# Expert layer in units of 32 rows on four column quarters of TensorE, where it was 64 rows on two column halves

## The reference, cut to what matters

```python
def moe_ffn(h, router_w, router_b, w_gate_up, b_gate_up, w_down, b_down):
    logits = (xt @ router_w + router_b)              # xt: 512 tokens x 1024
    top_v, top_i = lax.top_k(logits, TOP_K)          # 4 of 32 experts each
    gates = jax.nn.softmax(top_v, axis=-1)
...
    def expert_block(args):                          # for the rows of one expert
        gu = xb @ w_gate_up[e] + b_gate_up[e]        # 1024 -> 2048
        x_glu = jnp.minimum(gu[:, ::2], SWIGLU_LIMIT)
        x_lin = jnp.clip(gu[:, 1::2], -SWIGLU_LIMIT, SWIGLU_LIMIT)
        act = x_glu * jax.nn.sigmoid(SWIGLU_ALPHA * x_glu) * (x_lin + 1.0)
        return act @ w_down[e] + b_down[e]           # 1024 -> 1024
```

## Time and profile before

| | us |
|---|---|
| median of 3 runs | 1922.38 (1922.17 to 1924.41) |
| span of the profiled execution (first to last instruction) | 1919.6 |
| expert stage, from SP's first transfer in it to the last matmul's end | 360.7 to 1521.35 |
| PE busy in the span | 1788.8 |
| DVE, ACT, POOL busy | 1025.5, 795.8, 236.5 |

### The profile page before, as it was taken

One profiled execution on the slowest core, in us unless ns is written; L12 is line 12 of the kernel. 1 busy time (PEld: TensorE's weight loads), 2 busy tenths in 40 slices (PEclk: granted clock), 3 DMA queues, 4 the chain that ended last, 5 costly groups with the idle time before them and its releaser, 6 DMA issues. The chain is left out here.

```text
span 1919.6 us, 41921 instructions
## 1 busy us (share of the span) xinstructions
PE 1788.8 (93%) x14459; PEld 1106.8 (58%) x14459; DVE 1025.5 (53%) x1632; ACT 795.8 (41%) x1163; POOL 236.5 (12%) x302
## 2 busy tenths in 40 slices
PE   6999888599999999999999899999999769998897
PEld 3999654455555555555554455555555336777763
DVE  5794435554554555544544345545454473874655
ACT  5335523244444444444443344444444433533411
POOL 0000000111111111111111011111111220350000
PEclk9999999699999999999999899999999879999999
DMA  8881771449878997997599998999999662221011
GB/s 328 271 263 45 197 236 43 180 158 406 356 284 318 423 379 284 363 427 324 206 406 427 426 427 338 421 427 372 405 427 426 260 211 68 77 77 46 21 40 44
DMA packets 129708, 520.06 MB, mean 271 GB/s; under 512 B 13618, under 2 KB 52291, under 8 KB 80355
## 3 DMA queue, kind: packets, MB, share of 16 engines
q1 hardware_dynamic: 116754, 483.41, 64.3%
q0 software_dynamic: 12736, 35.17, 4.9%
q10 hardware_dynamic: 146, 0.48, 0.1%
HBM read 494.10 MB, written 24.90 MB: 270 GB/s over the span
## 5 line engine op out<-in xcount | busy, mean ns | idle before, releaser
L1893 DVE COPY ring<-staging 128x2048 f32 (+1 forms) x385 | 475.2, 1234 | 506.8 <-PE banks L1754 307.8
L1754 PE MATMUL banks<-ring,rowsT 128*64 128x256 f32 x6144 | 700.9, 381 | 3.2 <-ACT rowsT L1843 3.2
L1754 PEld LDWEIGHTS banks<-ring,rowsT 128*64 128x64 f32 x6144 | 443.4, 138 | 310.5 <-issue 78.7
L1825 ACT ACTIVATE ring<-staging 128x2048 f32 (+1 forms) x193 | 369.0, 1912 | 338.6 <-PE banks L1754 274.7
L1780 PE MATMUL banks<-ring,hiddenT 128*64 128x512 f32 x1536 | 375.4, 610 | 0.5 <-PEq L1811 0.3
L1780 PEld LDWEIGHTS banks<-ring,hiddenT 128*64 128x64 f32 x1536 | 93.7, 137 | 137.3 <-issue 113.0
L1831 ACT ACTIVATE glu<-banks 128x128 f32<-128x128 f32 x192 | 53.2, 277 | 281.5 <-DVE lin L1899 281.5
L601 PE MATMUL banks<-w_in_hi,hT 128*128 128x256 f32 (+1 forms) x768 | 147.3, 291 | 1.6 <-issue 1.6
L2227 PE MATMUL banks<-h3T,w_in_hi 128*128 128x512 f32 x400 | 130.5, 408 | 1.4 <-DVE h3T L2403 1.4
L601 PEld LDWEIGHTS banks<-w_in_hi,hT 128*128 128x128 f32 x768 | 122.5, 194 | 3.6 <-issue 3.5
L1707 POOL DMA_DIRECT2D expert_rows<-y_rows x94 | 52.4, 558 | 532.5 <-ACT y_rows L1849 531.5
(11 more groups left out here) (413 smaller groups left out, 1796.6 us busy)
## 6 DMA issues: line engine op xcount, KB each, us to landing
staging<-in_w_gate_up SPq DMA_DIRECT2D x250, 1024.0 KB, 12.6
staging<-in_w_down SPq DMA_DIRECT2D x128, 1024.0 KB, 12.6
stage<-in_w_mod SPq DMA_DIRECT2D x21, 1024.0 KB, 6.1
stage<-in_w_in SPq DMA_DIRECT2D x25, 512.0 KB, 4.1
expert_rows<-y_rows POOLq DMA_DIRECT2D x94, 128.0 KB, 5.8
stage<-in_w_in SPq DMA_DIRECT2D x11, 1024.0 KB, 6.2
expert_rows<-catT SPq DMA_DIRECT2D x1, 7936.0 KB
early<-in_w_gate_up SPq DMA_DIRECT2D x6, 1024.0 KB, 11.2
```

Of the source, the lines that this page charges most:

```text
L1754: mm = pe.matmul(k.bank(j % 2)[c * SLOTS:(c + 1) * SLOTS, 0:UP], rowsT[:, kk, half, :], w[:, kk * WIDE + c * UP:kk * WIDE + (c + 1) * UP], ...
L1825: act.activation(ring[:, pos % RING, :], staged(e, c), ACT.Copy).then_inc(act_filled, 1)
L1893: dve.tensor_copy(ring[:, pos % RING, :], staged(e, c)).then_inc(dve_filled, 1)
```

## The change

SLOTS goes from 64 to 32, so the counts above give 80 units: 6 experts with one, 14 with two, 7 with three, 2 with four, 2 with five, and one with seven. A unit's 32 rows stand on four groups of 32 array columns (`QUARTERS`); each quarter has a quarter of the output features, and reads its own quarter (`PART` = 512 floats) of every chunk. The weights are laid out anew on the host so that a chunk of gate and up holds 128 input features for all outputs, and chunks come in the order 0 to 7 (up), 8 to 11 (down). The down part of unit i - 1 now stands behind the whole up part of unit i. The hidden rows of a unit are made in one go, and the column that picks the expert's bias comes from the router (`k.lane`) instead of a load for each unit. POOL fetches rows two units ahead and no longer loads `picked`; its store is one transfer instead of two. The first expert's early chunks are copied to the ring from where they were loaded. SP's loads are written out one by one, without a loop. The router's one-hot matrices have 512 columns. `gate2` goes through HBM to make room.

The core of the diff:

```diff
-SLOTS = 64
+SLOTS = 32
+QUARTERS = 4
...
-BY_DVE = (0, 2, 3, 5, 6, 8, 9, 11)
-BY_ACT = (1, 4, 7, 10)
+BY_DVE = (0, 1, 3, 4, 6, 8, 9, 11)
+BY_ACT = (2, 5, 7, 10)
...
 # SP
+                def free(c, last):
+                    filled(sp, last if c < KT else last + 1, c)
...
 # POOL
                 def store_rows(n):
                     pool.wait_ge(y_read, n)
-                    for part in range(2):
-                        pool.dma_start(rows_of(part, n * SLOTS - SLOTS), y[part * SLOTS:(part + 1) * SLOTS, :]
-                                       ).then_inc(y_out, 16)
-                    pool.wait_ge(y_out, 32 * n)
+                    pool.dma_start(store_of(n * SLOTS - SLOTS), y[:]).then_inc(y_out, 16)
+                    pool.wait_ge(y_out, 16 * n)
                     pool.sem_inc(y_free, 1)
-                gather(0)
-                load_picked(0)
-                load_picked(1)
+                gather(0, y, 1)
                 gather(1)
+                gather(2)
                 with pool.Fori(1, units) as i:
-                    load_picked(i + 1)
-                    gather(i + 1)
+                    gather(i + 2)
                     store_rows(i)
...
 # PE
+                def up(i, qs=range(KT)):
...
+                        for c in range(QUARTERS):
+                            w = ring[:, q % RING, c * PART:(c + 1) * PART]
+                            mm = pe.matmul(k.bank(0)[c * SLOTS:(c + 1) * SLOTS, :], rowsT[:, q % 2, row], w,
...
+                with pe.Fori(1, units) as i:
+                    up(i)
+                    down(i - 1, i)
+                    turn_hidden(i)
+                    turn_rows(i + 2)
+                    add_bias(i + 1)
...
 # ACT
+                with act.Fori(1, units) as i:
+                    e = expert_on(act, i)
+                    fill(i, e, 5)
+                    fill(i, e, 7)
+                    fill(i, expert_on(act, i - 1), 10)
+                    gate(i)
+                    rows_turned(i + 1, i * CHUNKS + KT)
+                    fill(i + 1, expert_on(act, i + 1), 2)
+                    read_y(i - 1, i * CHUNKS + CHUNKS)
+                    hidden_turned(i)
...
 # DVE
+                with dve.Fori(1, units) as i:
+                    e = expert_on(dve, i)
+                    fill(i, e, 3)
+                    fill(i, e, 4)
+                    pick_expert(i + 1)
+                    fill(i, e, 6)
...
+                    fill(i, e_before, 8)
+                    fill(i, e_before, 9)
+                    linear(i)
+                    fill(i, e_before, 11)
+                    finish_hidden(i)
```

More of the change, by code:

```diff
@@ L41 @@
 TABLE = ENDS + NE + LINE
-UP = 2 * P
-NM = 8
 CHUNK = 2048
@@ L1673, in _ @@
[L1673 to L1679 removed]
+                up = lambda e, q: d["w_gate_up"][(e * KT + q) * P:(e * KT + q + 1) * P, :]
+                down = lambda e, m: d["w_down"][(e * 4 + m) * P:(e * 4 + m + 1) * P, :]
@@ new lines, in _ @@
+                for m in range(EARLY - AHEAD):
+                    arrived(m)
+                for m in range(EARLY, NE * CHUNKS):
+                    e, c = m // CHUNKS, m % CHUNKS
+                    old = m - STAGED
+                    if old >= 0:
+                        if old % CHUNKS == 0 or old == 0:
+                            of = old // CHUNKS
+                            last = sp.value_load(k.table[0:1, ENDS + of:ENDS + of + 1], min_val=0, max_val=NBLK - 1)
+                        free(old % CHUNKS, last)
+                    sp.dma_start(staging[:, m % STAGED * CHUNK:(m % STAGED + 1) * CHUNK],
+                                 up(e, c) if c < KT else down(e, c - KT)).then_inc(raw_in[m % STAGED], 16)
+                    arrived(m - AHEAD)
@@ L1811, in _, with add_bias @@
-                pe.sem_inc(chunk_done, 2)
-                down(end + 3, units, 3)
+                def add_bias(i):
+                    pe.wait_ge(pick_ready, i + 1)
+                    first = not (isinstance(i, int) and i == 0)
+                    if first:
+                        pe.wait_ge(lin_ready, i)
+                        pe.wait_ge(glu_ready, i)
+                    for part in range(2):
+                        mm = pe.matmul(k.bank(0), pick[:], bias[:, part, :], start=first and part == 0,
+                                       stop=not first and part == 1, skip_group_check=True)
+                    mm.then_inc(pick_used, 1)
@@ new lines, in turn_hidden, with down @@
+                def turn_hidden(i):
+                    pe.wait_ge(hidden_ready, i + 1)
+                    after(pe, hT_ready, i)
+                    for b in range(2):
+                        mm = pe.transpose(k.bank(2)[:, b * P:(b + 1) * P], hidden[:, b * P:(b + 1) * P], ident)
+                    mm.then_inc(turned_ps, 1)
+                def down(n, i):
+                    for m in range(4):
+                        if m == 0:
+                            pe.wait_ge(hT_ready, n + 1)
+                            after(pe, y_read, n)
+                        filled(pe, i, KT + m)
+                        for b in range(2):
+                            for c in range(QUARTERS):
+                                w = ring[:, (KT + m) % RING, c * PART + b * GLU:c * PART + (b + 1) * GLU]
+                                mm = pe.matmul(k.bank(4)[c * SLOTS:(c + 1) * SLOTS, 0:GLU],
+                                               hT[:, b, m * SLOTS:(m + 1) * SLOTS], w,
+                                               start=(m == 0 and b == 0), stop=(m == 3 and b == 1))
+                        mm.then_inc(chunk_done, 1)
@@ L1874, in _ @@
-                end = PAIRS * last
-                hidden_turned(end + 2, 2, last * CHUNKS + 9)
-                gate(end + 3, 3)
-                hidden_turned(end + 3, 3, units * CHUNKS)
+                act.activation(bias[:, 0, :], raw_bias, ACT.Copy).then_inc(bias_high, 1)
+                fill(0, 0, 5)
+                for m in (1, 3, 5):
+                    act.wait_ge(chunk_done, m + 1)
+                    act.activation(own_slot(m), k.early_slab(m), ACT.Copy).then_inc(settled, 1)
+                fill(0, 0, 7)
```

472 lines of the change are left out of this document (193 added, 279 removed).

## The result

The changed kernel takes 2140.42 us (2138.33 to 2141.86), the kernel before 1922.43: 1.1125 times as long, interval 1.1109 to 1.1142. That is 183 us over the forecast of 1957 and outside its range. The sign and the place were as forecast, the size was not.

What follows compares the result with a forecast made beforehand. PE bounds the expert stage now; after the change GpSimd's store-and-gather chain was expected to decide. Stage +26.4 us (1187 against 1160.6) and router +8 on 1922.4 gave 1957 us, range 1895 to 2010.

Steps and rivals of the forecast that it cites:

- PE, DVE and ACT: Expert stage, engine time per unit: four quarters at once, PE 11.6 us, DVE 11.3 at most, ACT 10.0; none over 11.6.
- (c): Quarters on PE overlap less than fully: 2000 us at a tenth less, 2560 at two at a time; chance 0.14.
- (d): DVE or ACT set the unit through waits in sequence: 12.6 us instead of 11.6, 1981 us; chance 0.18.
- The router and what is behind: Router before the expert stage: wider one-hot operations 4.3 us, last eight matmul records 3.4, with new transpose and copies +8.
- The loop: Chain through GpSimd of store, landing wait, gather and PE: 28.5 us per two units while loads queue, 23.1 otherwise.
- the store's landing: Wait in GpSimd's chain until a unit's store has landed: 6.0 us with the queue full, 2.9 when not.
- The gather: GpSimd's fetch of a unit's rows, at half the bytes: 6.4 us with the queue full, 4.1 with few loads.
- The rule of packets: DMA engines take a whole packet of one queue before the next; cited for a gather's 2.7 us behind queued loads.
- The clock: PE after waiting for a gather: 0.8 us for transposes, 10.6 for up and down parts; no slower clock included.
- The sum by experts: Expert stage: 612 us short experts, 312 and 281 for long experts' units, less 28 caught up, plus 10 start: 1187.
- The case without the loop: Expert stage if GpSimd's chain never binds: 612 + 46 x 11.6 - 28 + 10 = 1128 us.
- Rival (a): GpSimd's chain never binds because half-size transfers land in unloaded times; every unit 11.6 us, time 1898 us; chance 0.2.

Runs made afterwards that it cites:

- e8_even_store: Changed kernel, each unit's single store laid down as 128 pieces in a row, outermost dimension 128 instead of 4 (output not the reference's): 2030.9 us.
- e9_two_y: Changed kernel with the wait for a store's landing moved behind the next gather, and a second y buffer so gathers issue earlier: 1924.7 us.
- e13_two_y_no_loads: e9_two_y with each chunk load behind the first 16 cut to one partition (output not the reference's): 1723.9 us.
- e11_two_y_four: e9_two_y with each unit's store issued as four transfers of 32 rows by 256 columns: 1921.1 us, 0.9993 times the kernel before.
- e1_four_stores: Changed kernel with each unit's store as four transfers, one per quarter, the wait for landing where it stood: 2124.8 us.
- e3_y_first: Changed kernel with ScalarE reading y before it copies chunk 2 of the next unit into the ring: 2141.5 us.
- e17_store_twice: e4_no_loads with each unit's rows stored twice, one landing after the other, before GpSimd fetches again: 2033.4 us.
- e4_no_loads: Changed kernel with each chunk load behind the first 16 cut to one partition instead of 128 (output not the reference's): 1795.1 us.

## Why the prediction was wrong, step by step

- **PE, DVE and ACT: right.** Four quarters do run at once: the up part of a unit is 7.07 us for 4 x 3.62, the down part 3.64 for 4 x 1.94; a unit is 11.5 us for the 11.6 forecast, and rivals (c) and (d) are gone. The Trainium skill has 2.38 times for three column tiles (TensorE: Matmul & The Clock Gate, section "Measured speedup vs the span model"). That is no limit here: four halve what two took.
- **The router and what is behind: near in sum, not in its parts.** 5.9 us at the stage's start and 3.1 behind its end, for 8. The one-hot operations take 0.54 us for 0.41, so 2.1 us for the 4.3 taken; the last eight matmul records take 3.66 us for 3.78, where 3.4 more were put. And the run of the kernel before with cut loads starts its stage at 366.6, with the router as before, while what stands behind the stage takes 397.3 to 405.7 us over all runs: differences of 6 and 3 us are not sure to come from the change.
- **The loop: right in kind, 28.5 us forecast and 34.2 measured.** The step that failed is the store's landing: "two transfers of 64 rows now, one of 128 later: I take 6.0". It took 8.6. The form of the transfer had changed, 4x32x256 in the listing of the loop, and the forecast took from the diff only its rows and bytes. In e8_even_store, with a landing of 5.7 in the median, the time is 2030.9: this term, with what follows from it, is 1371.6 - 1265.4 = 106.2 us of the stage. The gather was right: 6.24 us for 6.4. Behind a full queue it lands some 3 us later than without (medians of 6.7 and 3.4 over the gathers above 5.5 and below 4.6 us), as it did with twice the bytes (2.7), so fewer bytes do not shorten that wait. The rule of packets that the prediction puts beside the 2.7 us is no explanation of it: the loads' packets in 743.5:753 hold 7.4 KB (3.47 MB in 469), and by that rule fewer bytes would have fewer packets to wait for.
- **The clock: left out.** PE behind a wait was costed at 11.4 us (0.8 and 10.6) as if it had not waited. The rows show 14.0 us (761.69 to 772.07 + 3.63) where it is 11.3 without a wait (775.90 to 783.57 + 3.64). With the slower turnaround of GpSimd (11.68 us from the store to the next gather, less 8.6 for the landing, is 3.1; the forecast put 2.1, and its named parts, 0.8 and 1.02, make 1.8) this is the next part: e8_even_store lies 1265.4 - 1163.4 = 102.0 us over e9_two_y, which has no such waits, where the forecast gave the loop 1187 - 1128 = 59. That is 43.0 us. How they divide between clock, turnaround and the rest wasn't measured. What the clock costs in all can be read across the three terms, and is no fourth one: for the same matmuls PE is busy 1052.8 us in the stage of the changed kernel (361:1738, granted clock 0.85), 1038.5 in e8_even_store (0.89), 1016.6 in e9_two_y (0.91) and 935.7 in e13_two_y_no_loads (0.99). The forecast had 80 x 11.6 = 928, at full clock throughout.
- **The sum by experts: too low.** The case without the loop was put at a stage of 1128 us; e9_two_y has 1163.4: 35.4 us. Cut at the ends of the up parts, its 20 short experts take 551.1 us, less than the forecast's 612 - 28: what was to be given back is there. But the 11 long experts behind the first take 527.3 us and not 41 x 11.6 = 475.6: six of them, each behind a short one, last 7 to 11 us longer, and the sum had given the loads no time there. The first expert takes 75.0 us for 68.0, and the 10.0 us from the last up part's end to the last down part's were in no term of the sum. The three terms are the whole miss of the stage, because they are differences from run to run: 106.2 + 43.0 + 35.4 = 184.6 = 1371.6 - 1187. The border between the last two is as uncertain as the stage of e9_two_y, some 7 us.
- **Rival (a) had the wrong end too.** Stores and gathers that never bind do not give 1898 us but about 1921 (e11_two_y_four): the change takes 1115 us of PE time down to 920, and the loads, 967 us, which ran beside PE almost for nothing before, now take turns with it. That the 16 staging places are what makes them take turns is argued from SP's 310 us of waiting for a place in e9_two_y, and not shown: SP waits 343.7 us for a place in the kernel before too, and no run had more places.

## What to carry to other kernels

Read the shape of each transfer in a diff as closely as its bytes: what its outermost dimension is, how many issues it takes, and only then how much it moves. Where a wait for a landing stands between two issues of one queue, look for the loop through it, and try the wait one issue later before anything else: here one moved line was worth 206 us. A unit made shorter gives back only what its companion allows: with both PE and loads near the stage's length, measure each without the other first.

## What the runs showed of the hardware that was not expected

- The same 128 KB in the same 128 pieces: 4.2 us with an outermost dimension of 4, 2.1 with 128, and 8.6 against 5.7 in the median.
- GpSimd needs 3.1 us in the median to issue four transfers of 32 KB (e1_four_stores), 0.76 for one of 128 KB, and up to 1.8 for that one while VectorE copies (e3_y_first).
- A wait of PE of 0.58 us left its clock alone, one of 5.44 us cost 1.8 us of work at a lower clock, one of 8.3 us 2.7 (a granted clock of 0.50 in the 3.8 us behind it). Over a stage, 172.0 us more of such waits made PE's same work 58.7 us longer (e17_store_twice against e4_no_loads).
